# Shifting the SBUF buffers of a two-layer decoder kernel by 64 bytes

## The chip, the cores and the metric

The kernel runs on one NeuronCore of a Trainium2 chip. Its time is the device time of one execution in microseconds (us). Three executions of the kernel before gave 1855.04, 1858.58 and 1860.55 us, so the median to compare with is 1858.58 us. On-chip memory is SBUF, 128 partitions side by side; an "address" below is a byte offset within every partition, and the "place" of a buffer is its address modulo 512.

## The reference

The kernel computes a two-layer decoder trunk for one sequence of 512 tokens with model width 1024, in float32:

```python
for l in range(DEPTH):                      # DEPTH = 2
    x = x + 0.5 * swiglu(rms_norm(x, g_ffn1[l]), w_ffn1_gate[l], w_ffn1_up[l], w_ffn1_down[l])
    h = rms_norm(x, g_mix[l])
    if l % 2 == 0:
        x = x + conv_gating_mixer(h, ...)   # 31-tap causal conv, LayerNorm, 128x128 spatial mixing, w_out
    else:
        x = x + stick_breaking_mixer(h, w_qkv[i], w_o[i])   # 16 heads of 64
    x = x + 0.5 * swiglu(rms_norm(x, g_ffn2[l]), w_ffn2_gate[l], w_ffn2_up[l], w_ffn2_down[l])
return rms_norm(x, g_final)

def swiglu(h, w_gate, w_up, w_down):        # 1024 -> 2816 -> 1024
    return (jax.nn.silu(h @ w_gate) * (h @ w_up)) @ w_down
```

So the work is four feed-forward blocks (FFN 0 to 3) with a convolution/gating mixer between 0 and 1 and an attention mixer between 2 and 3.

## The kernel before, in words

Activations lie transposed (feature on the partition, token along the row). Every float32 matrix product is made of three products in the type fp32r: high part times high part, high times low, low times high. ScalarE (ACT) makes the high parts and VectorE (DVE) the low parts; GpSimd (POOL) and DMAs that add on landing form sums of weight blocks.

The gate and up products of an FFN are done with seven products in place of eight (a Strassen-like scheme). One of 11 steps handles seven items (`T1` to `T4`), each with three passes of eight matmuls of 256 columns: line 654 in `gate_pass`, 168 matmuls a step. The weights come from a ring of four slots, `w_hi` and `w_lo`, the moving operand from `xs_hi` and `xs_lo`. The down product and the mixers' products use matmuls of 512 columns. In the helper `three` (lines 447 to 449) the three parts follow each other; in `pair_added` (L828), `v_added` (L842) and `project` (L994) all of one part come first. In most of them weight tiles are loaded into TensorE from `w_hi`/`w_lo` and activations (`xs`, `xg`, `a`, `v_cat`) stream past. For the values of the mixers (`v_added`, `v_chunk`) it is the other way round: `xg` is loaded, and `w_hi`/`w_lo` stream. Attention uses `qk` against `qk` (scores), `keep` against the constants `neg_tri` and `neg_ones` (suffix sums), and `prob` against `v_cat`.

While one matmul streams, the next weight tile is loaded ("PEld" in the profile). TensorE's order is written out by hand, the same for every run, and waits on semaphores only at the heads of items.

Buffers are put into SBUF one behind the other as a stack in the order of the `sb(...)` calls (lines 119 to 199), each rounded up to 32 bytes; a scope that closes gives its room back. The places are therefore set by the sizes of the small buffers ahead of them. `x_res`, `stage`, `w_hi` and `w_lo` come first and lie at place 128. The small buffers `tok_rms`, `tok_rinv`, `params`, `taps`, `eps_col` and `eps_root` have sizes that are no multiples of 512 and move everything behind them.

Of the kernel before, what the change touches and what calls it, by code (L numbers as in the profile page):

```python
# [6 lines left out]
F32R = mybir.dt.float32r  # L7
# [4 lines left out]
P = 128  # L12
S = 512
D = 1024
DT = D // P
TT = S // P
# [4 lines left out]
CT = CA // P  # L21
TAPS = 31
PAD = TAPS - 1
GB = 4
# [82 lines left out]
def trunk_kernel(nc, x, g_ffn1, w_ffn1_gate, w_ffn1_up, w_ffn1_down, g_mix, w_in_ab, conv_w, conv_b,  # L107
# [3 lines left out]
    with ctx:  # L111
        def sb(name, shape, dt=F32, scope=ctx):
            return scope.enter_context(nc.sbuf_tensor(name, shape, dt))
# [10 lines left out]
        ssq = sb("ssq", [P, S])  # L124
        rms = sb("rms", [P, S])
        rinv = sb("rinv", [P, S])
        tok_rms = sb("tok_rms", [P, TT])
        tok_rinv = sb("tok_rinv", [P, TT])
        ones = sb("ones", [P, P])
        neg_ones = sb("neg_ones", [P, P], F32R)  # L130
        neg_tri = sb("neg_tri", [P, P], F32R)
        ident = sb("ident", [P, P])
        params = sb("params", [P, PARAM_ROWS])
        taps = sb("taps", [P, TAPS * CT])
        eps_col = sb("eps_col", [P, 1])
        eps_root = sb("eps_root", [P, 1])
        ps = ctx.enter_context(nc.psum_tensor("ps", [P, 8, 512], F32))


# [15 lines left out]
        xg_hi = sb("xg_hi", [P, DT, S], F32R, mixer_scope)  # L155
        xg_lo = sb("xg_lo", [P, DT, S], F32R, mixer_scope)
        with ExitStack() as conv_scope:
            a_pad = sb("a_pad", [P, CT, PAD + S], scope=conv_scope)
            y = sb("y", [P, CT, S], scope=conv_scope)
            v_mean = sb("v_mean", [P, TT, GB], scope=conv_scope)  # L160
            v_stat = sb("v_stat", [P, TT, GB], scope=conv_scope)
            v_rstd = sb("v_rstd", [P, TT, GB], scope=conv_scope)
            rinv2 = sb("rinv2", [P, TT], scope=conv_scope)
            g_buf = sb("g_buf", [P, 2, S], scope=conv_scope)
            sp_rows = sb("sp_rows", [P, GB, P], scope=conv_scope)
            sp_hi = sb("sp_hi", [P, GB, P], F32R, conv_scope)
            sp_lo = sb("sp_lo", [P, GB, P], F32R, conv_scope)
            sp_bias = sb("sp_bias", [P, GB, P], scope=conv_scope)
            sp_shift = sb("sp_shift", [P, GB, P], scope=conv_scope)
            taps_hi = sb("taps_hi", [P, TAPS], F32R, conv_scope)  # L170
            taps_lo = sb("taps_lo", [P, TAPS], F32R, conv_scope)


            u = sb("u", [P, GB, S], scope=conv_scope)
            v_cen = sb("v_cen", [P, TT, GB, P], scope=conv_scope)
            v_n_hi = sb("v_n_hi", [P, TT, S], F32R, conv_scope)
            v_n_lo = sb("v_n_lo", [P, TT, S], F32R, conv_scope)
            b_hi, b_lo = xg_hi[:, 0:GB, :], xg_hi[:, GB:2 * GB, :]
            with ExitStack() as late_scope:
                a_pad_hi = sb("a_pad_hi", [P, PAD + S], F32R, late_scope)  # L180
                a_pad_lo = sb("a_pad_lo", [P, PAD + S], F32R, late_scope)
                diags = [sb(f"diags_{part}", [P, PE_TAPS, P], F32R, late_scope) for part in ("hi", "lo")]
            a_hi = sb("a_hi", [P, CT, S], F32R, conv_scope)
            a_lo = sb("a_lo", [P, CT, S], F32R, conv_scope)
# [2277 lines left out]
```

## Time and profile before

| | |
|---|---|
| median of three executions | 1858.58 us (1855.04 to 1860.55) |
| the profiled execution, own time | 1852.68 us |
| its span (first to last instruction) | 1850.9 us |
| TensorE (PE) busy | 1818.5 us, 98% |
| weight loads (PEld) busy | 1626.7 us, 88% |
| DVE busy | 1416.0 us, 77% |
| ACT busy | 929.0 us, 50% |
| POOL busy | 512.3 us, 28% |
| mean granted TensorE clock | 0.998 |

"Busy" for TensorE counts a matmul from its start until its result has left the array. Matmuls overlap in this pipeline, so a mean duration of 279 ns for 256 columns does not say how fast they follow each other. What one costs in a row of many is the distance between starts, which one gets from the time stamps and the counts in the rows below. In a row's names, `ps<-xs_hi,w_hi`, the output stands before the arrow, then the moving operand and then the loaded one.

### The profile page before, as it was taken

How to read it: one execution, taken by the hardware profiler on the slowest of the kernel's cores; microseconds unless marked ns; L12 is line 12 of the kernel's file. 1: busy time of each engine (PE TensorE's matmuls, PEld its weight loads, DVE VectorE, ACT ScalarE, POOL GpSimd, SP SyncE). 2: the span in 40 equal slices, each digit the busy share in tenths (PEclk: the TensorE clock that was granted, in tenths of full speed). 3: DMA queues.
4: the chain of work that ended last, by engine and by line, in shares of the span. 5: the costliest groups of instructions: out<-in, count | busy, mean ns of one | idle time of the engine just before them, and what ended most of it. 6: DMA issues, size and time to landing. Idle time of an engine off the chain costs nothing.

```text
span 1850.9 us, 29139 instructions
## 1 busy us (share of the span) xinstructions
PE 1818.5 (98%) x11672; PEld 1626.7 (88%) x11672; DVE 1416.0 (77%) x1320; ACT 929.0 (50%) x1095; POOL 512.3 (28%) x395
## 2 busy tenths in 40 slices
PE   8999999999999999999999999999999999999998
PEld 7999988888799999888999988888888889999786
DVE  7888886599887888855888895654777698888753
ACT  6455444356374554444545453424666475545442
POOL 4433302311023333001344410220443233343021
PEclk9999999999999999999999999999999999999999
DMA  9887643265568876426887842222332287886321
GB/s 241 189 208 172 154 131 91 80 172 137 124 154 189 206 179 149 136 91 148 184 197 188 192 138 93 90 91 68 88 84 79 69 188 183 200 191 166 114 85 46
DMA packets 230025, 262.98 MB, mean 142 GB/s; under 512 B 8020, under 2 KB 196000, under 8 KB 227888
## 3 DMA queue, kind: packets, MB, share of 16 engines
q1 hardware_dynamic: 179232, 195.58, 34.3%
q0 software_dynamic: 50592, 66.14, 22.2%
q8 instruction: 61, 1.00, 0.2%
q14 instruction: 28, 0.23, 0.0%
q10 hardware_dynamic: 112, 0.03, 0.0%
HBM read 240.75 MB, written 2.10 MB: 131 GB/s over the span
## 4 chain that ended last, share of the span: by engine, by line
PE 67%; DMA 11%; DVE 10%; issue 5%; ACT 4%; POOL 2%; DVEq 0%; SPq 0%; ACTq 0%; POOLq 0%
PE ps L654 21%; PE ps L447 12%; PE ps L448 11%; PE ps L449 11%; DMA stage<-in_w_ffn_gate_dram 9%; PE ps L994 4%; DVE w_lo L1701 4%; PE ps L828 2%; POOL chain L2325 1%; ACT w_hi L1184 1%; PE ps L842 1%; PE ps L1025 1%; PE ps L1031 1%; PE ps L1045 1%; DMA hid<-hid 1%
## 5 line engine op out<-in xcount | busy, mean ns | idle before, releaser
L1701 DVE TENSOR_TENSOR w_lo<-stage,w_hi 128x1024 fp32r<-128x1024 f32 x261 | 423.4, 1634 | 27.3 <-ACT w_hi L1184 26.7
L654 PE MATMUL ps<-xs_hi,w_hi 128*128 128x256 f32 x2432 | 335.1, 279 | 7.9 <-ACT w_hi L1184 6.2
L654 PE MATMUL ps<-xs_lo,w_hi 128*128 128x256 f32 x2432 | 332.5, 278 | 2.1 <-DVE xs_lo L1914 1.9
L654 PE MATMUL ps<-xs_hi,w_lo 128*128 128x256 f32 x2432 | 332.5, 278 | 0.0
L654 PEld LDWEIGHTS ps<-xs_hi,w_hi 128*128 128x128 f32 x2432 | 304.1, 188 | 12.4 <-issue 5.4
L654 PEld LDWEIGHTS ps<-xs_lo,w_hi 128*128 128x128 f32 x2432 | 303.5, 188 | 2.9 <-DVE xs_lo L1914 2.5
L654 PEld LDWEIGHTS ps<-xs_hi,w_lo 128*128 128x128 f32 x2432 | 303.5, 188 | 0.3
L447 PE MATMUL ps<-xs_hi,w_hi 128*128 128x512 f32 x704 | 278.8, 396 | 3.5 <-issue 2.9
L448 PE MATMUL ps<-xs_lo,w_hi 128*128 128x512 f32 x704 | 278.2, 395 | 0.0
L449 PE MATMUL ps<-xs_hi,w_lo 128*128 128x512 f32 x704 | 278.1, 395 | 0.0
L1184 ACT ACTIVATE w_hi<-chain 128x1024 fp32r<-128x1024 f32 x129 | 136.5, 1061 | 225.6 <-POOL chain L2325 121.5
L1833 DVE TENSOR_TENSOR xs_lo<-hid,xs_hi 128x1024 fp32r<-128x1024 f32 x88 | 110.6, 1256 | 176.0 <-ACT xs_hi L1333 176.0
L1184 ACT ACTIVATE w_hi<-stage 128x1024 fp32r<-128x1024 f32 x173 | 178.2, 1054 | 102.0 <-DMA stage<-in_w_ffn_gate_dram 50.7
L1333 ACT ACTIVATE xs_hi<-hid 128x1024 fp32r<-128x1024 f32 x88 | 93.3, 1060 | 263.9 <-PE ps L449 254.8
L1701 DVE TENSOR_TENSOR w_lo<-chain,w_hi 128x1024 fp32r<-128x1024 f32 x129 | 156.3, 1218 | 63.8 <-ACT w_hi L1184 61.8
L2319 POOL TENSOR_TENSOR chain<-chain,stage 128x1024 f32<-128x1024 f32 x40 | 96.4, 2411 | 293.4 <-DVE w_lo L1701 293.4
L447 PEld LDWEIGHTS ps<-xs_hi,w_hi 128*128 128x128 f32 x704 | 132.1, 188 | 37.7 <-issue 5.8
L449 PEld LDWEIGHTS ps<-xs_hi,w_lo 128*128 128x128 f32 x704 | 132.2, 188 | 32.0
L448 PEld LDWEIGHTS ps<-xs_lo,w_hi 128*128 128x128 f32 x704 | 132.2, 188 | 31.5
L2325 POOL TENSOR_TENSOR chain<-chain,stage 128x1024 f32<-128x1024 f32 x43 | 124.6, 2898 | 94.3 <-DVE w_lo L1701 94.3
L2294 POOL TENSOR_TENSOR sq<-x_res 128x512 f32<-128x512 f32 x23 | 34.2, 1489 | 342.4 <-DVE x_res L1687 341.1
L2306 POOL DMA_DIRECT2D chain<-in_w_ffn_gate_dram x43 | 56.3, 1309 | 135.7 <-DMA chain<-in_w_ffn_up_dram 135.6
(260 smaller groups left out, 2639.2 us busy)
## 6 DMA issues: line engine op xcount, KB each, us to landing
stage<-in_w_ffn_up_dram SPq DMA_DIRECT2D x88, 512.0 KB, 4.0
stage<-in_w_ffn_gate_dram SPq DMA_DIRECT2D x88, 512.0 KB, 5.2
stage<-in_w_ffn_down_dram SPq DMA_DIRECT2D x88, 512.0 KB, 3.8
chain<-in_w_ffn_gate_dram POOLq DMA_DIRECT2D x46, 512.0 KB, 7.3
stage<-in_w_ffn_gate_dram POOLq DMA_DIRECT2D x44, 512.0 KB, 6.9
chain<-in_w_ffn_up_dram SPq DMA_DIRECT2D x43, 512.0 KB, 6.3
w_lo<-stage POOLq DMA_DIRECT2D x12, 1024.0 KB, 7.2
stage<-in_w_qkv_dram SPq DMA_DIRECT2D x24, 512.0 KB, 4.7
```

The source lines that it names most:

```text
L447: pe.matmul(to, a_hi, b_hi, start=start, stop=False, skip_group_check=True)
L448: pe.matmul(to, a_hi, b_lo, start=False, stop=False, skip_group_check=True)
L449: return pe.matmul(to, a_lo, b_hi, start=False, stop=stop, skip_group_check=True)
L654: mm = pe.matmul(ps[:, bank + BANK_OF[item], t * HS:(t + 1) * HS], w[:, slot, (2 * k + t) * P:(2 * k + t + 1) * P], xs[:, PART_OF[item], k ...
L994: mm = pe.matmul(ps[:, 6, :], tile(slot, (n % 2) * DT + k)[part // 2], (xg_lo if part == 1 else xg_hi)[:, k, :], start=(part == 0 and k == ...
L1184: act.activation(w_hi[:, slot, :], raw(n, step, item), ACT.Copy).then_inc(item_hi_made, split_counts(n, step, item))
L1333: act.activation(xs_hi[:, PART_S2 + e % 2].rearrange("p k c -> p (k c)"), hid[:, 2 * pair:2 * pair + 2, :].rearrange("p a s -> p (a s)"), ...
L1701: return dve.tensor_tensor(w_lo[:, slot, :], src, w_hi[:, slot, :].bitcast(F32), ALU.subtract)
L1833: dve.tensor_tensor(xs_lo[:, part].rearrange("p k c -> p (k c)"), hid[:, 2 * pair:2 * pair + 2, :].rearrange("p a s -> p (a s)"), xs_hi[:, ...
L2306: pool.dma_start(step.chain().rearrange("p (k f) -> p k f", k=KH), gate_block(n, T3, step), accum_op=ALU.add).then_inc(t1_made, 16)
L2319: pool.tensor_tensor(step.chain(), step.chain(), raw(n, step, W22), ALU.add).then_inc(t2_made, 1)
L2325: pool.tensor_tensor(raw(n, step, T4), raw(n, step, T4), raw(n, step, W21), ALU.add).then_inc(t4_made, 1)
```

## The change

No instruction is added, removed or moved: on each of the five engines the sequence of instructions is the same as before. Only addresses change. The four 128x128 constants now stand before `tok_rms` and `tok_rinv`; a filler `line` of 64 bytes that nothing uses follows `eps_root`; in the convolution's scope the buffers with odd sizes (`a_pad`, `v_mean`, `v_stat`, `v_rstd`, `rinv2`, `taps_hi`, `taps_lo`) are put behind the large ones, with a second filler `conv_line`.

```diff
@@ -124,16 +124,18 @@
-        tok_rms = sb("tok_rms", [P, TT])
-        tok_rinv = sb("tok_rinv", [P, TT])
         ones = sb("ones", [P, P])
         neg_ones = sb("neg_ones", [P, P], F32R)
         neg_tri = sb("neg_tri", [P, P], F32R)
         ident = sb("ident", [P, P])
+        tok_rms = sb("tok_rms", [P, TT])
+        tok_rinv = sb("tok_rinv", [P, TT])
         params = sb("params", [P, PARAM_ROWS])
         taps = sb("taps", [P, TAPS * CT])
         eps_col = sb("eps_col", [P, 1])
         eps_root = sb("eps_root", [P, 1])
+
+        sb("line", [P, 16])
@@ -155,26 +157,25 @@
         with ExitStack() as conv_scope:
-            a_pad = sb("a_pad", [P, CT, PAD + S], scope=conv_scope)
             y = sb("y", [P, CT, S], scope=conv_scope)
-            v_mean = sb("v_mean", [P, TT, GB], scope=conv_scope)
...
             v_n_lo = sb("v_n_lo", [P, TT, S], F32R, conv_scope)
+            a_pad = sb("a_pad", [P, CT, PAD + S], scope=conv_scope)
+            v_mean = sb("v_mean", [P, TT, GB], scope=conv_scope)
...
+            sb("conv_line", [P, 16], scope=conv_scope)
```

The places, as the allocator gives them, and the distance "moving minus loaded" modulo 512 of each kind of matmul. Every slice that these matmuls take begins at a multiple of 512 bytes within its buffer (but for the taps), so a buffer's place is that of all its tiles.

| matmuls | columns | places before: moving, loaded | distance before | distance after |
|---|---|---|---|---|
| gate (L654): `xs`, `w` | 256 | 64, 128 | -64 | 0 |
| down: `xs`, `w` | 512 | 64, 128 | -64 | 0 |
| mixers: `xg` or `v_cat`, `w` | 512 | 64, 128 | -64 | 0 |
| values (L842, `v_chunk`): `w`, `xg` | 512 | 128, 64 | +64 | 0 |
| mixer: `a_hi`/`a_lo`, `w` | 512 | 0, 128 | -128 | 0 |
| scores: `qk`, `qk` | 128 to 512 | 64, 64 | 0 | 0 |
| suffix: `keep`, `neg_tri`/`neg_ones` | 128 to 512 | 64, 192 | -128 | 0 |
| `prob`, `v_cat` | 128 to 512 | 64, 64 | 0 | 0 |
| spatial mixing: `sp`, `v_n` | 128 | 256, 0 | 256 | 0 |
| taps: `a_pad_hi`/`lo` shifted by 4k, `diags` | 512 | 0/128 + 4k, 256 | varies | the same |

For the vector engines, `chain` (place 64 before, 128 after) joins `stage` and `w_hi`, which lie at 128 both before and after.

## Rows read from the trace of the kernel before

**Rows 1.** The page: busy time, share and count of TensorE.
```profile
PE 1818.5 (98%) x11672; PEld 1626.7 (88%) x11672; DVE 1416.0 (77%) x1320; ACT 929.0 (50%) x1095; POOL 512.3 (28%) x395
```
**Rows 2.** Groups of TensorE's matmuls by form: count | busy us, mean ns | idle.
```profile
L654 PE MATMUL ps<-xs_hi,w_hi 128*128 128x256 f32 x2432 | 335.1, 279 | 7.9 <-ACT w_hi L1184 6.2 <-ACT copies L1224 1.0 <-ACT copies L1217 0.4
L447 PE MATMUL ps<-xs_hi,w_hi 128*128 128x512 f32 x704 | 278.8, 396 | 3.5 <-issue 2.9 <-DVE xs_lo L1833 0.2
L447 PE MATMUL ps<-xg_hi,w_hi 128*128 128x512 f32 x96 | 38.9, 405 | 0.0
L994 PE MATMUL ps<-xg_hi,w_hi 128*128 128x512 f32 x112 | 29.2, 402 | 0.0
L447 PE MATMUL ps<-v_cat,w_hi 128*128 128x512 f32 x64 | 26.0, 406 | 1.3 <-DVE v_cat L2177 0.7 <-DVE w_lo L1672 0.3 <-DVE x_res L1687 0.3
L447 PE MATMUL ps<-w_hi,xg_hi 128*128 128x512 f32 x64 | 25.1, 392 | 0.0
L828 PE MATMUL ps<-xg_hi,w_hi 128*128 128x512 f32 x48 | 12.1, 403 | 0.0
L842 PE MATMUL ps<-w_hi,xg_hi 128*128 128x512 f32 x32 | 7.8, 394 | 0.0
```
**Rows 3.** Two stretches of 100 us, line 654 alone: matmuls in brackets, clock.
```profile
100.00:200.00 100.00, 100.00 (x852) 100.00 (x851) 1.00 0.80 190
980.00:1080.00 100.00, 100.00 (x885) 100.00 (x884) 1.00 0.77 178
```
**Rows 4.** The chain that ended last: start us, us, what.
```profile
387.93 22.41 PE ps L828 x96
410.78 22.00 PE ps L842 x96
543.48 21.15 PE ps L654 x184
585.31 9.80 DMA stage<-in_w_ffn_gate_dram
596.32 138.79 PE ps L654 x1176
888.96 21.14 PE ps L654 x184
```
**Rows 5.** Groups in the stretches 57:228, 596.3:746.5 and 873.4:888.5 us, line 654.
```profile
L654 PE MATMUL ps<-xs_hi,w_hi 128*128 128x256 f32 x481 | 67.2, 282 | 0.9 <-ACT w_hi L1184 0.9
...
L654 PE MATMUL ps<-xs_hi,w_hi 128*128 128x256 f32 x427 | 59.2, 281 | 1.2 <-ACT w_hi L1184 1.2
...
L654 PE MATMUL ps<-xs_hi,w_hi 128*128 128x256 f32 x48 | 7.4, 281 | 0.0
```
**Rows 6.** Timeline of the weight loads in one head's scores: start us, duration.
```profile
1376.99 0.19 PEld L448 LDWEIGHTS ps<-qk_lo,qk_hi 64*128 64x128 f32 x1
1377.22 0.18 PEld L449 LDWEIGHTS ps<-qk_hi,qk_lo 64*128 64x128 f32 x1
1377.46 0.18 PEld L447 LDWEIGHTS ps<-qk_hi 64*128 64x128 f32 x1
...
1378.23 0.18 PEld L448 LDWEIGHTS ps<-qk_lo,qk_hi 64*128 64x128 f32 x1
1378.35 0.18 PEld L449 LDWEIGHTS ps<-qk_hi,qk_lo 64*128 64x128 f32 x1
1378.46 0.18 PEld L447 LDWEIGHTS ps<-qk_hi 64*128 64x128 f32 x1
```
**Rows 7.** DVE's line 1701 by operands: count: duration ns min/median/max.
```profile
L1701 DVE TENSOR_TENSOR w_lo<-stage,w_hi x261: 1209/1220/3460, 26.6 to 1816.3; 128x1024 fp32r<-128x1024 f32 x131
L1701 DVE TENSOR_TENSOR w_lo<-chain,w_hi x129: 1209/1217/1228, 37.2 to 1704.4; 128x1024 fp32r<-128x1024 f32 x129
```

More of the change, by code:

```diff
@@ L157, in trunk_kernel @@
         with ExitStack() as conv_scope:
-            a_pad = sb("a_pad", [P, CT, PAD + S], scope=conv_scope)
             y = sb("y", [P, CT, S], scope=conv_scope)
-            v_mean = sb("v_mean", [P, TT, GB], scope=conv_scope)
-            v_stat = sb("v_stat", [P, TT, GB], scope=conv_scope)
-            v_rstd = sb("v_rstd", [P, TT, GB], scope=conv_scope)
-            rinv2 = sb("rinv2", [P, TT], scope=conv_scope)
             g_buf = sb("g_buf", [P, 2, S], scope=conv_scope)
@@ L169, in trunk_kernel @@
             sp_shift = sb("sp_shift", [P, GB, P], scope=conv_scope)
-            taps_hi = sb("taps_hi", [P, TAPS], F32R, conv_scope)
-            taps_lo = sb("taps_lo", [P, TAPS], F32R, conv_scope)
             u = sb("u", [P, GB, S], scope=conv_scope)
@@ L177, in trunk_kernel @@
             v_n_lo = sb("v_n_lo", [P, TT, S], F32R, conv_scope)
+            a_pad = sb("a_pad", [P, CT, PAD + S], scope=conv_scope)
+            v_mean = sb("v_mean", [P, TT, GB], scope=conv_scope)
+            v_stat = sb("v_stat", [P, TT, GB], scope=conv_scope)
+            v_rstd = sb("v_rstd", [P, TT, GB], scope=conv_scope)
+            rinv2 = sb("rinv2", [P, TT], scope=conv_scope)
+            taps_hi = sb("taps_hi", [P, TAPS], F32R, conv_scope)
+            taps_lo = sb("taps_lo", [P, TAPS], F32R, conv_scope)
+            sb("conv_line", [P, 16], scope=conv_scope)
             b_hi, b_lo = xg_hi[:, 0:GB, :], xg_hi[:, GB:2 * GB, :]
```

## The prediction
> **What bounds the kernel now.** I read the page first: TensorE is busy for 1818.5 of 1850.9 us [rows 1], so all its idle time together is 32 us, and no other engine is above 77%. Only the rate at which matmuls follow each other, or those 32 us, can give time back. The change touches no instruction and so no wait; what it can touch is the rate. Then the groups by form, for the counts: the gate products are three groups of 2432 matmuls of 256 columns, the down products three of 704 with 512 columns [rows 2]. Their mean durations (279, 396 ns) overlap and are no price.
>
> So I took distances between starts. Two stretches of 100 us in which line 654 runs without a break hold 852 and 885 matmuls, both at a clock of 1.00: 117.4 and 113.0 ns each [rows 3]. The same instructions with the same distance of operands (-64) thus run at two rates, 4.4 ns apart. The chain of waits shows when the rate changes. In FFN 1, 184 matmuls take 21.15 us (114.9 ns, restarts included); then comes a wait for a DMA, and the next 1176 take 138.79 us, 118.0 ns each, to the end of the loop without recovering. In FFN 2 it goes the other way [rows 4]. A rate is kept until a stall, and the restart draws it anew. At full clock 256 columns are 106.7 ns, so both rates carry an excess, of about 7 and 11 ns, that belongs to no wait.
>
> For 512 columns the chain has two kinds side by side: L828 (distance -64) 96 in 22.41 us, 233.4 ns; L842 (distance +64) 96 in 22.00 us, 229.2 ns [rows 4]. That is 4.2 ns for what differs between them: which operand is loaded, the line, and the distance. It is the one hint in this trace that place counts at all.
>
> **The change part by part.**
>
> (a) Gate products, 7296 matmuls (3 x 2432), distance -64 to 0. The slow stretches hold x481, x427 and x48 of the first of three passes [rows 5]; the other two passes have 480 and 480, 424 and 424, 40 and 40, together 2844 matmuls. The other 4452 are in the quick rate or in restarts. If distance 0 always settles in the quick rate: 2844 x 4.4 ns = 12.5 us less. If it always settles in the slow one: 4452 x 4.4 = 19.6 us more. No long row of 256-column matmuls at distance 0 exists in this trace, so these are my bounds. I take -12.5: the quick rate is the one reached more often under the present distance, and I assume that starting both streams at one place removes whatever keeps them locked in the slower pattern. That is an assumption, and the weakest one here.
>
> (b) Products of 512 columns at distance -64: 3 x (704 + 96 + 112 + 64 + 48) = 3072 [rows 2]. At L842's price they would save 4.2 ns each, 12.9 us. At the price of the 512-column scores, whose distance is 0 already, they would save nothing: there the loads start at 1376.99, 1377.22 and 1377.46 us, 230 and 240 ns apart [rows 6], 235 on average and no better than 233.4. The scores use 64 rows and are short chains, but they are the nearest rows for distance 0. I take nothing, and keep -12.9 for the range.
>
> (c) Values at distance +64, 3 x (64 + 32) = 288 matmuls at 229.2 ns [rows 2, 4]: at 233.4 they would cost 1.2 us more. I take 0, with +1.2 as the other end. The 96 matmuls of `a`, the suffix sums and the 48 of the spatial mixing are at most 4 ns x some 500, 2 us either way; taken as 0. The taps keep their distance.
>
> (d) The vector engines. L1701 subtracts `w_hi` (place 128) from `stage` (128) in a median of 1220 ns and from `chain` (64) in 1217 ns [rows 7]: equal places cost DVE 3 ns. On 129 instructions that is 0.4 us, on an engine that sits idle 23% of the span beside a TensorE that is 98% busy. 0 on the path. If DVE's cover were gone, it would be 0.4 us. DMAs keep their counts, sizes and start at multiples of 64 bytes as before; 0, bounded by TensorE's 32 us of idle time, of which a tenth, 3 us, is what I would allow for a shift.
>
> Sum: -12.5 us. On the profiled execution, 1852.68 - 12.5 = 1840.2 us. That execution was 5.9 us under the median of the runs, so against the median of 1858.6 it is 1846.1; I say 1846. About 5.6 us (0.3%) is what a measurement can tell from no change.
>
> A rule speaks against any effect. Rows 4 show two prices for 512 columns, 233.4 and 229.2 ns. The Trainium skill (TensorE: Matmul & The Clock Gate, Step-by-step: what each phase is for) says that TensorE reads SBUF through two independent ports, one for the moving operand and one for the weight loads. By it the place of one relative to the other would mean nothing and the sum would be 0; that is rival 2 below, whose price and chance come from rows 3 and 4. The same page (Back-to-back issue gap) gives an isolated gap of N/2.4 + 2.5 ns, about 216 ns for 512 columns, where the rows have 233.4: this trace does not agree, something beyond the rule costs 17 ns. Were all of that excess removed on the 3072 matmuls, it would be an estimate by that page of 54 us; I do not use it.
>
> **The rivals.**
>
> 1. Place counts for all lengths: the gates all quick and the 512s at L842's price. -12.5 - 12.9 = -25.4, so 1833 us. For: L828 and L842 differ by a constant 4.2 ns in neighbouring stretches. Against: the scores at distance 0 show 230 to 240 ns. Chance 0.15.
>
> 2. Place does not count. Each restart draws the rate again, since DMA landings vary from run to run. Three runs before lie within 5.5 us, so whole FFNs seldom flip between runs of one kernel; but a kernel with other addresses may draw differently. One FFN's loop of eight steps with 168 matmuls each is 1344 x 4.4 = 5.9 us. Time 1858.6, mostly within 6 us of it. For: both rates occur at one distance. Chance 0.27: 0.18 within 0.3%, 0.05 faster, 0.04 slower.
>
> 3. Slower: distance 0 locks the gates in the slow rate. Loads and stream then start together in one place, and stay beside each other; the place is every item of L654 in FFN 2 and 3 (and the starts of 0 and 1). Price 19.6 + 1.2 = 20.8 us, 1879 us, from the point where more than 2844 of the 7296 gate matmuls, 39%, run slow. For: the 256-column scores at distance 0 follow each other by 110 to 120 ns [rows 6], nearer 117 than 113, and the 512-column ones show no gain. Against: these are three in a row right after another length, and short rows after a restart are slow at distance -64 too before they settle. Chance 0.28.
>
> **How the numbers follow.** Forecast 0.30, rival 1 0.15, rival 2 0.27, rival 3 0.28. Faster by over 0.3%: 0.27 of the forecast (0.03 for gains that come out under 5.6 us), 0.15, 0.05: 0.47. Same: 0.03 + 0.18 = 0.21. Slower: 0.28 + 0.04 = 0.32. The range runs from 1830 (rival 1 less the 3 us of (d)) to 1878, about the end of rival 3, of which half, 0.14, is left out. The forecast's own range is 1838 to 1852.
>
> **What would show it right or wrong.** Right for (a): every stretch of 100 us inside the gate loops, those of FFN 0 and 1 too, holds some 885 matmuls. The slow lock would show as 852 in all four. Rival 2 would show both counts again, in whichever FFNs. For (b): L828's 96 matmuls again in 22.4 us; 22.0 or less would be rival 1. For (c): L842 stays near 22.0. For (d): the median of both kinds of L1701 stays at 1217 to 1220 ns, and TensorE's idle time at about 32 us; if that grows by more than 5 us, waits have moved and the whole sum is about the wrong thing. The forecast is wrong if a gate loop of FFN 0 or 1 still runs at 117 ns.

## Result and profile after

The changed kernel is slower. Twenty-two runs of each give medians of 1860.12 us (1858.37 to 1862.80) for the changed kernel and 1855.19 us (1841.17 to 1866.25) for the kernel before. The ratio is 1.0034, 95% interval 1.0019 to 1.0049, that is 3.5 to 9.1 us more. The forecast of 1846 us, 12.5 us less than the kernel before, had the wrong sign; the time lies in the range of 1830 to 1878. The changed kernel's runs spread over 4.4 us, those of the kernel before over 25 us.

The profiled execution took 1858.50 us, its span 1856.8 us, 5.9 us more than before. The page's line on TensorE, which answers to [rows 1]:

```profile
PE 1831.2 (99%) x11672; PEld 1660.5 (89%) x11672; DVE 1419.6 (76%) x1320; ACT 927.1 (50%) x1095; POOL 498.3 (27%) x395
```

TensorE is busy 12.7 us longer, and idle 1856.8 - 1831.2 = 25.6 us where it was idle 32.4. The stretches of line 654 (now L655), in the columns of [rows 3]:

```profile
100.00:200.00 100.00, 100.00 (x836) 100.00 (x835) 1.00 0.80 189
980.00:1080.00 100.00, 100.00 (x836) 100.00 (x835) 1.00 0.77 178
```

Both hold 836 matmuls, and so does 600:700 us: a third rate, 119.6 ns, where before there were 852 and 885. The timeline (start us, length, count) shows it without the rounding at a stretch's ends:

```profile
1003.43 1.12 PE L655 MATMUL ps<-xs_hi,w_hi 128*128 128x256 f32 x8
1004.39 1.12 PE L655 MATMUL ps<-xs_lo,w_hi 128*128 128x256 f32 x8
1005.35 0.88 PE L655 MATMUL ps<-xs_hi,w_lo 128*128 128x256 f32 x6
```

The starts of two groups of eight are 0.96 us apart, 120.0 ns each. The 512-column products went the other way. The chain, beside [rows 4], then a stretch of the down product of FFN 2 (TensorE alone; first the kernel before, then after), then the timeline of L829:

```profile
386.40 21.76 PE ps L829 x96
408.60 21.81 PE ps L843 x96
```
```profile
1120.00:1200.00 80.00, 80.00 (x344) 1.00 0.27 83
```
```profile
1120.00:1200.00 80.00, 80.00 (x354) 1.00 0.24 74
```
```profile
389.86 3.79 PE L829 MATMUL ps<-xg_lo,w_hi 128*128 128x512 f32 x16
393.49 3.79 PE L829 MATMUL ps<-xg_hi,w_lo 128*128 128x512 f32 x16
397.12 3.79 PE L829 MATMUL ps<-xg_hi,w_hi 128*128 128x512 f32 x16
```

Main and swapped roles now take the same time (21.76 and 21.81 us for 96), and starts lie 3.63 / 16 = 226.9 ns apart, where L828 had 233.4.

**Where the time went**, from these rows: 2844 gate matmuls from 117.4 to 119.6 ns and 4452 from 113.0 to 119.6 ns, +35.6 us. 3072 products of 512 columns, 80 us / 344 against 80 us / 354, 6.6 ns each, -20.3 us. 288 values from 229.2 to 227.2 ns, -0.6 us. TensorE's idle time, -6.8 us. The sum is +7.9 us for a measured +5.9. Of the 2 us left over the 96 `a` products can make 0.5 (5.5 ns each), and the rounding of the counts the rest: one matmul more or less in a stretch of 100 us is 0.14 ns, 1 us over 7296. The gates' +35.6 us belong to this pair of profiles, in which the kernel before had two slow loops and two quick ones.

### The profile page after: what moved, and what is told of

The parts are those of the page before. It is cut to its first block, busy times and chain, and to the rows that moved or that the text cites. A ratio compares the mean times of both kernels' runs of the same rounds, so it can differ in the third digit from the quotient of the medians.

```text
span 1856.8 us, 29139 instructions
## 1 busy us (share of the span) xinstructions
PE 1831.2 (99%) x11672; PEld 1660.5 (89%) x11672; DVE 1419.6 (76%) x1320; ACT 927.1 (50%) x1095; POOL 498.3 (27%) x395
## 3 DMA queue, kind: packets, MB, share of 16 engines
q1 hardware_dynamic: 179232, 195.58, 34.3%
## 4 chain that ended last, share of the span: by engine, by line
PE 84%; DVE 7%; ACT 3%; DMA 2%; issue 2%; POOL 1%; DVEq 0%; ACTq 0%; POOLq 0%
PE ps L655 39%; PE ps L448 11%; PE ps L450 11%; PE ps L449 11%; PE ps L995 4%; DVE w_lo L1702 2%; DMA stage<-in_w_ffn_gate_dram 2%; PE ps L829 2%; PE ps L843 1%; PE ps L1026 1%; PE ps L1032 1%; PE ps L1046 1%; DVE xs_lo L1834 1%; DVE rinv L1692 1%; POOL chain L2326 1%
## 5 line engine op out<-in xcount | busy, mean ns | idle before, releaser
L1702 DVE TENSOR_TENSOR w_lo<-stage,w_hi 128x1024 fp32r<-128x1024 f32 x261 | 449.2, 1733 | 37.1 <-ACT w_hi L1185 37.0
L655 PE MATMUL ps<-xs_hi,w_hi 128*128 128x256 f32 x2432 | 346.4, 284 | 4.3 <-ACT w_hi L1185 3.0
L655 PE MATMUL ps<-xs_lo,w_hi 128*128 128x256 f32 x2432 | 344.2, 283 | 0.6 <-DVE xs_lo L1915 0.4
L655 PE MATMUL ps<-xs_hi,w_lo 128*128 128x256 f32 x2432 | 343.8, 283 | 0.0
L655 PEld LDWEIGHTS ps<-xs_hi,w_hi 128*128 128x128 f32 x2432 | 315.0, 192 | 8.5 <-ACT w_hi L1185 4.0
L655 PEld LDWEIGHTS ps<-xs_lo,w_hi 128*128 128x128 f32 x2432 | 314.7, 192 | 1.4 <-DVE xs_lo L1915 0.9
L655 PEld LDWEIGHTS ps<-xs_hi,w_lo 128*128 128x128 f32 x2432 | 314.8, 192 | 0.0
L449 PE MATMUL ps<-xs_lo,w_hi 128*128 128x512 f32 x704 | 273.9, 389 | 0.0
L1185 ACT ACTIVATE w_hi<-chain 128x1024 fp32r<-128x1024 f32 x129 | 135.9, 1057 | 226.9 <-PE ps L655 107.0
L1702 DVE TENSOR_TENSOR w_lo<-chain,w_hi 128x1024 fp32r<-128x1024 f32 x129 | 156.5, 1217 | 75.0 <-ACT w_hi L1185 74.4
L2320 POOL TENSOR_TENSOR chain<-chain,stage 128x1024 f32<-128x1024 f32 x40 | 95.8, 2396 | 310.8 <-DVE w_lo L1702 303.5
L448 PEld LDWEIGHTS ps<-xs_hi,w_hi 128*128 128x128 f32 x704 | 132.2, 188 | 32.1 <-issue 5.1
L450 PEld LDWEIGHTS ps<-xs_hi,w_lo 128*128 128x128 f32 x704 | 132.2, 188 | 27.6
L449 PEld LDWEIGHTS ps<-xs_lo,w_hi 128*128 128x128 f32 x704 | 132.2, 188 | 27.0
L2326 POOL TENSOR_TENSOR chain<-chain,stage 128x1024 f32<-128x1024 f32 x43 | 111.4, 2590 | 93.8 <-DVE w_lo L1702 93.8
L2313 POOL DMA_DIRECT2D stage<-in_w_ffn_gate_dram x44 | 57.2, 1299 | 143.4 <-DMA stage<-in_w_ffn_gate_dram 143.4
```

Of the source, the lines that this page charges most:

```text
L448: pe.matmul(to, a_hi, b_hi, start=start, stop=False, skip_group_check=True)
L449: pe.matmul(to, a_hi, b_lo, start=False, stop=False, skip_group_check=True)
L450: return pe.matmul(to, a_lo, b_hi, start=False, stop=stop, skip_group_check=True)
L655: mm = pe.matmul(ps[:, bank + BANK_OF[item], t * HS:(t + 1) * HS], w[:, slot, (2 * k + t) * P:(2 * k + t + 1) * P], xs[:, PART_OF[item], k ...
L1185: act.activation(w_hi[:, slot, :], raw(n, step, item), ACT.Copy).then_inc(item_hi_made, split_counts(n, step, item))
L1702: return dve.tensor_tensor(w_lo[:, slot, :], src, w_hi[:, slot, :].bitcast(F32), ALU.subtract)
```

## The experiments

Theories: **D**, the rate of a row of matmuls depends on the columns of each matmul and on the distance between the streaming and the loaded operand; **P**, the place of the streaming operand alone counts; **L**, each restart draws a rate whatever the layout; **W**, the time went into waits or the vector engines. All kernels below are edits of the changed kernel, but for the one that repeats the kernel before. mixers_at_0, split and split_m48 have six to twelve runs, the others one each, so of the others the rates are compared and not the times: the kernel before by itself had medians of 1855.19, 1845.39 and 1851.19 us in three sessions. Windows rows are of line 655, or of that line's number in the edited kernel.

**d_plus64.**
```diff
-        sb("line", [P, 16])
+        sb("line", [P, 32])
```


> The changed kernel with its filler of 64 bytes made 128, so that the streaming operands lie 64 bytes beyond the loaded ones (distance +64 in place of 0; the values of the mixers, where the roles are swapped, get -64). Theory D (the rate depends on the distance of the two operands modulo 512 and on the length alone): the 512-column products take 229 ns each, as the values did at +64 in the kernel before, and the values (L843) 233.4 ns. Theory P (the place of the streaming operand alone counts): the values, whose streaming operand stays at place 128, keep the 226.7 ns of the changed kernel. Theory L (a draw at each restart): gate products change their rate between stretches, 113 or 118 ns, whatever the distance. For the gates D names no number, only one that is steady or, as at -64, one of two.

Windows, then chain:
```profile
980.00:1080.00 100.00, 100.00 (x885) 100.00 (x884) 1.00 0.75 177
1600.00:1700.00 100.00, 100.00 (x851) 100.00 (x851) 1.00 0.76 179
```
```profile
387.67 21.97 PE ps L829 x96
410.08 22.40 PE ps L843 x96
```
The two kinds of products have changed sides: 228.9 ns for the main ones at +64, 233.3 for the values at -64. P falls, since the values' streaming operand stayed at place 128 and its distance between starts rose from 227.2 to 233.3 ns. The gates have both rates again, 885 and 851. The single time was 1853.79 us.

The down products at +64, which the chain rows above do not hold, do not keep to one rate either. FFN 1, then FFN 2, TensorE alone:
```profile
780.00:860.00 80.00, 80.00 (x351) 1.00 0.42 119
1120.00:1200.00 80.00, 80.00 (x344) 1.00 0.30 92
```
By recorded starts those of FFN 0, 1 and 3 follow each other by 228.9 ns and those of FFN 2 by 233.3. So at +64 the 512-column products have two rates as well, and D's 229 ns is only one of them. FFN 2 is the one whose gates ran quick here; whether the two belong together, one run cannot tell.

**d_plus128** (`[P, 48]`).

> The same with a filler of 192 bytes, distance +128, values -128. D: the values (L843) take about 232.2 ns, as the products of a_hi and a_lo did at -128 in the kernel before. P: the values stay at 226.7 ns. If the cost comes from two streams that meet in one part of a 512-byte line, 256 columns should cost no more than 120 ns.

```profile
980.00:1080.00 100.00, 100.00 (x845) 100.00 (x844) 1.00 0.77 178
```
```profile
390.12 22.31 PE ps L829 x96
412.87 22.30 PE ps L843 x96
```
The values take 232.3 ns, as D says (232.2). Gates are at 118.3 ns. Both roles agree, so +128 and -128 cost the same.

**d_plus256** (`[P, 80]`).

> The same with a filler of 320 bytes, distance 256 for both roles: half a line, the farthest from equal places. D: main products and values have the same rate, since +256 and -256 are the same place modulo 512. P: they differ unless the place does not count.

```profile
980.00:1080.00 100.00, 100.00 (x836) 100.00 (x835) 1.00 0.76 178
```
```profile
386.90 21.76 PE ps L829 x96
409.10 21.81 PE ps L843 x96
```
This is the changed kernel over again, count for count. At 256 bytes, the farthest place modulo 512, nothing differs from equal places, so the period looks like 256 bytes and not 512. By it +128 and -128 have to be alike, which d_plus128 and d_minus128 bear out, and +64 and -64 need not be.

**d_minus128** (`[P, 112]`).

> The same with a filler of 448 bytes, distance -128, values +128. D: the 512-column products take 232.2 ns as those of a_hi did before; the values take the rate that the main products show at +128. P: the values stay at 226.7 ns.

```profile
980.00:1080.00 100.00, 100.00 (x845) 100.00 (x844) 1.00 0.77 178
```
```profile
388.53 22.30 PE ps L829 x96
411.27 22.30 PE ps L843 x96
```
232.3 ns for main products and for values, gates 118.3 ns: equal to +128, as a period of 256 bytes has it. Time 1868.64 us.

**before_again**, no edit.

> The kernel before, unchanged, profiled once more. Its times spread from 1841 to 1866 us over 22 runs, those of the changed kernel only from 1858 to 1863. Theory D+L (at distance -64, i.e. 192 modulo 256, the gate products have two steady rates, 113.3 and 117.8 ns, and a restart draws one): other stretches than before are slow this time, and the span differs from 1850.9 us by 4.4 ns times the change in slow matmuls. If the layout alone set the rate in each stretch, the same stretches would be slow (FFN 0 and 1, start of FFN 2) and the span would be within 2 us of 1850.9.

```profile
100.00:200.00 100.00, 100.00 (x885) 100.00 (x884) 1.00 0.84 195
600.00:700.00 100.00, 100.00 (x885) 100.00 (x884) 1.00 0.84 199
```
In the first profile these two stretches held 852 and 851; the span fell from 1850.9 to 1842.7 us. One kernel, two draws. Over all its gate matmuls the mean distance between starts fell from 115.2 to 114.0 ns, 9 us for 7296, of which waits took back 2. So L holds, but only at distances with two steady rates (-64, +64, and -48 in split_m48 below); at 0 and 256 no gate loop left 120.0 ns.

**d_plus32** (`[P, 24]`) and **d_minus32** (`[P, 8]`).

> The changed kernel with a filler of 96 bytes: distance +32, half way between 0 (gates 120.0, 512 columns 226.7 ns) and +64 (116.8 on average, 230.2). If the cost changes gradually with distance: 118 to 119 and 228 to 229 ns. If only the 64-byte unit in which an address lies counts, +32 behaves as 0 or as +64 to within 0.5 ns.

> The changed kernel with a filler of 32 bytes: distance -32, between 0 (120.0, 226.7 ns) and -64 (115.2 on average, 233.4). Gradual: about 117 and 230 ns. By 64-byte units: as 0 or as -64.

For +32, then for -32:
```profile
980.00:1080.00 100.00, 100.00 (x851) 100.00 (x851) 1.00 0.77 179
```
```profile
388.40 22.40 PE ps L829 x96
```
```profile
980.00:1080.00 100.00, 100.00 (x848) 100.00 (x847) 1.00 0.76 178
```
```profile
389.70 22.40 PE ps L829 x96
```
The gradual guess fails at both. 512 columns take 233.3 ns at both, more than at 0 or at +64; the gates take 117.5 and 117.9 ns. The guess by 64-byte units fails at +32, which takes 512 columns neither as 0 nor as +64 does; at -32 both prices are close to the slow ones of -64, but no loop runs quick. For 512 columns 32 bytes off 0 the gain is gone. Times: 1868.08 and 1871.04 us.

**shift_all.**
```diff
+        sb("ahead", [P, 16])
         x_res = sb("x_res", [P, DT, S])
```


> The changed kernel with 64 bytes put ahead of x_res, so that loaded and streaming operands move together: distance 0, all places 192 in place of 128. Theory D (distance): gates 120.0 ns, 512 columns 226.7 ns, as in the changed kernel. Theory P (absolute place): both change by nanoseconds. Span within 3 us of 1856.8 by D.

```profile
980.00:1080.00 100.00, 100.00 (x836) 100.00 (x835) 1.00 0.76 178
```
```profile
389.73 21.77 PE ps L830 x96
411.94 21.79 PE ps L844 x96
```
The places of weights and activations are both 192 and the rates are those of the changed kernel: at distance 0 a common shift of 64 bytes changes nothing. With the exchange of roles in d_plus64 this speaks for the distance and against the place of either operand alone. The span, 1860.9 us, is 4.1 us longer where 3 were allowed. The rates do not explain that, half of it is idle time (27.6 us for 25.6), and the time of 1862.60 us lies within the changed kernel's own 1858.37 to 1862.80.

**mixers_at_0.**
```diff
-        sb("line", [P, 16])
...
         mixer_scope = ExitStack()
+        sb("line", [P, 16], scope=mixer_scope)
```


> The changed kernel with its 64-byte filler moved into the mixers' scope: operands of the mixers keep distance 0, those of the four FFNs go back to -64. Theory D (a price by distance and length): mixers' 512-column products 226.7 ns, down products 233.4, gates at 113.3 or 117.8 by the draw (114.0 and 115.2 on average in the two profiles of the kernel before). Against the kernel before that is 960 x 6.7 + 288 x 2.5 + 96 x 5.5 ns = 7.7 us less, so 1847 us beside a median of 1855. Theory W (the change cost time through waits or the vector engines and not through the gates): about as the changed kernel, 1860.

Chain, then windows:
```profile
380.63 21.76 PE ps L829 x96
402.83 21.81 PE ps L843 x96
```
```profile
600.00:700.00 100.00, 100.00 (x885) 100.00 (x884) 1.00 0.84 195
980.00:1080.00 100.00, 94.80 (x837) 94.60 (x835) 1.00 0.71 174
```
1840.04 us against 1845.39 for the kernel before on that chip, ratio 0.998 (0.996 to 0.9999): 0.2 to 7.4 us less where 7.7 were expected. The rates are as D says; the size expected lies just outside the interval, and a draw at the gates is part of both medians. W, which expected the time of the changed kernel, falls. The second stretch shows a limit: TensorE is busy 94.8 of 100 us there, so gates at the quick rate (113.3 ns) meet waits.

**split.**
```diff
-            xs_hi = sb("xs_hi", [P, 7, KH, HS], F32R, ffn_scope)
-            xs_lo = sb("xs_lo", [P, 7, KH, HS], F32R, ffn_scope)
+            xs_hi_all = sb("xs_hi", [P, 7 * KH * HS + 64], F32R, ffn_scope)
+            xs_lo_all = sb("xs_lo", [P, 7 * KH * HS + 16], F32R, ffn_scope)
+            xs_hi, xs_lo = [t[:, 0:7 * KH * HS].rearrange("p (q k c) -> p q k c", q=7, k=KH) for t in (xs_hi_all, xs_lo_all)]
...
+        def down_half(of, e):
+            at = (PART_S2 + e % 2) * KH * HS + 16
+            return of[:, at:at + KH * HS]
...
-                    act.wait_ge(item_used, USED0[n] + GATE_ITEMS - ITEMS + T2 + 1 + e)
+                    act.wait_ge(item_used, USED0[n] + GATE_ITEMS - ITEMS + T2 + 2)
```
on top of mixers_at_0, with `down_half` wherever the down product's activations are written or read. The 64 columns added to `xs_hi` put `xs_lo` 256 bytes further, so its distances are 192 for the gates and 256 for the down products; by the period of 256 bytes that is -64 and 0. By recorded starts the passes with `xs_lo` run like those with `xs_hi` (114.8 and 114.9 ns on average, 227.0 and 226.8), a second sign of that period.

> Each product at its better distance: gates at -64, mixers at 0, and the down products at 0 too, because the hidden activations are written 64 bytes further within the same buffer (with a wait that is one item longer for the first of them). D: gates 113.3 or 117.8 ns, down and mixers 226.7 ns; against the kernel before 7.7 us and another 2112 x 6.7 ns = 14.2 us less, 1833 us. W: no better than the kernel before, 1855 or more.

Page, a down stretch, two gate stretches:
```profile
PE 1795.1 (98%) x11672; PEld 1624.0 (89%) x11672; DVE 1407.3 (77%) x1320; ACT 927.0 (51%) x1095; POOL 519.4 (28%) x395
```
```profile
1120.00:1200.00 80.00, 80.00 (x354) 1.00 0.28 87
```
```profile
100.00:200.00 100.00, 100.00 (x851) 100.00 (x850) 1.00 0.79 187
600.00:700.00 100.00, 100.00 (x885) 100.00 (x884) 1.00 0.84 195
```
1827.16 us (1825.03 to 1832.44) against 1845.39, ratio 0.9899 (0.9877 to 0.9921), 14.6 to 22.7 us less; 21.9 were expected. The down stretch has the 354 of distance 0 and the gates the two rates of -64, in one kernel. It beats the kernel before. The changed kernel was not run on that chip; its fastest run elsewhere was 1858.37 us, split's slowest 1832.44. The one wait that is an item longer was not tried alone.

**wlo_64.** The filler of 64 bytes stands ahead of `w_lo` in place of behind `eps_root`.

> The changed kernel with the filler of 64 bytes moved ahead of w_lo: w_hi and the activations stay at place 128, w_lo goes to 192, so only loads of low weights have the distance -64. Theory N (a stream is slowed by the load of the next tile that runs beside it): in the down products the matmul ahead of the one that uses w_lo (the one that streams the low activations against w_hi) is the one that changes, the other two stay near 226.7 ns. Theory O (a stream is slowed by its own tile's place): the matmul that uses w_lo changes. In the gates, whose low-weight pass is 8 matmuls in a row, that pass leaves 120.0 ns for 113 to 118 by D, the other two passes stay at 120.0 ns; average 118.

```profile
980.00:1080.00 100.00, 100.00 (x841) 100.00 (x841) 1.00 0.77 178
```
In the down products the means between recorded starts are 228.5 ns after `xs_hi,w_hi`, 229.2 after `xs_lo,w_hi` and 235.6 after `xs_hi,w_lo`. The largest change is at the matmul that uses `w_lo`, as O says, but the two others rose by 2 ns too, and in the record the next tile's load starts with the stream. So this does not decide between O and N. Longer rows keep D's prices by pass. The timeline of the mixer's products (16 in a row), then of the gates (8 in a row):
```profile
393.03 3.79 PE L829 MATMUL ps<-xg_lo,w_hi 128*128 128x512 f32 x16
396.65 3.89 PE L829 MATMUL ps<-xg_hi,w_lo 128*128 128x512 f32 x16
400.38 3.82 PE L829 MATMUL ps<-xg_hi,w_hi 128*128 128x512 f32 x16
```
```profile
1003.19 1.12 PE L655 MATMUL ps<-xs_lo,w_hi 128*128 128x256 f32 x8
1004.15 1.11 PE L655 MATMUL ps<-xs_hi,w_lo 128*128 128x256 f32 x8
1005.09 1.12 PE L655 MATMUL ps<-xs_hi,w_hi 128*128 128x256 f32 x8
```
The pass with `w_lo`, at -64, takes 3.73 us for 16 and 0.94 us for 8; the passes with `w_hi`, at 0, take 3.62 and 0.96. So the gate pass with `w_lo` leaves 120.0 ns for 117.9 on average and the two others stay, as expected; all together 118.9 ns by the count.

**split_m48.** In split, `t[:, 0:7 * KH * HS]` becomes `t[:, 4:7 * KH * HS + 4]`.

> The kernel split, with the gates' view of the activations 16 bytes further: gates at distance -48 in place of -64, down products and mixers still at 0. If the two rates of the gates at -64 belong to the exact tie of 64-byte steps, -48 shows one rate; by the trend from -32 (118.3 ns on average) to -64 (113.8 to 115.2) it lies near 116.5 ns, 7296 x 1.7 to 2.7 ns = 12 to 20 us more than split, 1839 to 1847. If 16 bytes are enough to keep the quick rate and lose the slow one: 113.3 ns always and 1825 or less.

```profile
600.00:700.00 100.00, 100.00 (x842) 100.00 (x841) 1.00 0.80 187
980.00:1080.00 100.00, 100.00 (x860) 100.00 (x859) 1.00 0.75 177
```
1854.89 us against 1851.19, ratio 1.001 (0.9992 to 1.0028): both expectations missed. The gates have 842 and 860, 118.8 and 116.3 ns, so there are two rates at -48 too, both slower than the quick one of -64. By this comparison, on another chip, 16 bytes cost all that split had gained.

| distance (modulo 256) | gates, 256 columns, ns | 512 columns, ns |
|---|---|---|
| 0 | 119.6 (120.0 by starts) | 226.7 |
| +32 | 117.5 | 233.3 |
| +64 | 113.0 or 117.5 | 228.9, in one loop 233.3 |
| 128 | 118.3 | 232.3 |
| -64 | 113.0 or 117.4 | 233.4 |
| -48 | 116.3 or 118.8 | not run |
| -32 | 117.9 | 233.3 |

The gates' prices are 100 us divided by the count, which takes in matmuls cut by the ends of a stretch; by recorded starts they are 0.3 to 0.5 ns higher (120.0 at 0, 118.7 at 128, 117.8 at +32, 118.3 at -32, 113.3 or 117.8 at +64 and -64). In the rows of +32, -32 and -48 the activations also start at a place that is no multiple of 64 bytes, which is so in none of the others. No run has such a start at distance 0 or 64, so what the distance does there and what the start does is not separated. The absolute place is excluded for shifts of 64 bytes alone.

## Why the prediction was wrong

**Step (a), the gates, failed.** It took the two rates at distance -64, 117.4 and 113.0 ns, as the bounds for distance 0, and of these the quick one. Distance 0 has a rate of its own, slower than both, that no row of before showed in a long run. The term was put between -12.5 and +19.6 us; it came out at +35.6. The assumption named as the weakest, that starting both streams in one place would free the quick rate, was half right: it removes the draw (d_plus256, shift_all and the changed kernel have one rate in every loop, and the times spread over 4.4 us), but in favour of a slow one.

**Step (b), 512 columns, failed in size.** Nothing was taken, with -12.9 us as the other end; the runs show -20.3. The bound from L842 was too narrow, because that line stood at +64 and not at 0: d_plus64 shows the same 228.9 ns at +64 for the main products, outside FFN 2, and 0 is 2 ns better. The reading that counted against a gain was that of the scores, 235 ns at distance 0 [rows 6]. They still run so after the change, in the same short chains on 64 rows, and were no sample of a long chain on 128 rows; which of the two matters was not tried. Rival 1 had this term with the right sign, and the gates' with the wrong one.

**Step (c)** expected 0 to +1.2 us for the values; they gained 0.6, as the same good place holds for swapped roles.

**Step (d)** held for the vector engine and not for the waits. L1702 has medians of 1219 and 1215 ns for its two kinds of operands. TensorE's idle time, for which 3 us either way were allowed, fell by 6.8. It goes with the speed of the gates: 29.5 to 34.3 us in the five profiles in which at least one gate loop ran at 113 ns (32.4 before, 34.3 in before_again, 31.5 in split), 23.5 to 28.9 in the nine others (25.6 here, 23.8 in d_plus256). That slower gates leave the transfers more time would explain it, but that is argued and not tested.

**Rival 3** had the sign and the place, gates locked in a slow rate, at +20.8 us: its 19.6 for the gates are 16 us too little, and it lacked the 20.3 us that the long products gave back. **Rival 2** is refuted as a statement on place, yet its draw is real at -64 (before_again). Its premise that whole FFNs seldom flip, from three runs within 5.5 us, did not last: 22 runs lie within 25 us. The Trainium skill's statement on two independent read ports (TensorE: Matmul & The Clock Gate, Step-by-step: what each phase is for) does not cover this case: with shift_all at equal rates and d_plus64 exchanging them between roles, the place of one operand relative to the other matters by up to 7 ns a matmul.

**Open** is what the two reads collide in. At distance 0 the excess over the streamed columns is the same for both lengths: 120.0 ns are 288 cycles at 2.4 GHz, 256 + 32; 226.7 ns are 544, 512 + 32. At -64 it is 16 cycles (113.3 ns by the distances of starts) or about 27 (117.8 ns) for 256 columns and 48 (233.4 ns) for 512. One fixed stall per matmul at distance 0 fits these numbers; that it comes from the load of a tile beside the stream is only argued, and wlo_64 did not settle beside which load.

## What to carry to other kernels

When TensorE is busy throughout, count the matmuls in equal stretches, in every loop: one kernel can hold several steady rates, and each length of matmul may want its own distance between streamed and loaded operand. Of the distances tried here equal places modulo 256 bytes were best for 512 columns (226.7 ns against 233.4) and worst for 256 (120.0 against 113.3 or 117.8), so one shift of the activations against the weights moved 36 us one way and 20 us the other; giving each product its own distance was worth 1.0%. A rate in short chains, or at a neighbouring distance, is no bound for a long chain at the new one: try it first.

## What the runs showed of the hardware

- The rate of these fp32r matmuls changes with the distance of the two operands' SBUF addresses. It is the same at distances 0 and 256 and with both operands shifted by 64 bytes (836 matmuls per 100 us in all three), and at +128 and -128 (845).
- At distance -64 and +64 a row of 256-column matmuls has two steady rates, 885 or 851 to 852 per 100 us at the same granted clock of 1.00, and which one a loop has changes after waits [rows 4] and from run to run (before_again). 512-column products at +64 had 228.9 ns in three loops and 233.3 in one (d_plus64). Two profiles of the kernel before that differ in two such loops have spans 8.2 us apart; that the draw is all of its spread of 25 us was not shown.
- At +32 and -32 bytes 96 matmuls of 512 columns take 22.40 us, at 0 21.76.
